# Expert weights by halves over 21 places, one buffer of gathered tokens, and a new order at the start of the expert stage

## The reference

```
h = rms_norm(x, norm_ffn)
choose one of 4 groups by router, in it 2 of 8 experts   # 32 experts in all
for each expert e, for the tokens that chose it:
    y = (silu(h @ w_gate[e]) * (h @ w_up[e])) @ w_down[e]  # 1024 -> 512 -> 1024
x = x + sum over the two experts of weight * y
x = rms_norm(x, norm_final)
```

## Time and profile before

| | |
|---|---|
| median of 3 runs | 964.09 us |
| the profiled execution | 965.7 us |
| its span, first to last instruction | 964.5 us |
| granted TensorE clock over the span | 0.993 |
| PE busy | 927.3 us, 96% |
| DVE, ACT busy | 455.5 us, 356.7 us |
| bytes moved by DMA | 291.88 MB, 303 GB/s over the span |

### The profile page before, as it was taken

One profiled execution on the slowest core, in us unless ns is written; L12 is line 12 of the kernel. 1 busy time (PEld: TensorE's weight loads), 2 busy tenths in 40 slices (PEclk: granted clock), 3 DMA queues, 4 the chain that ended last, 5 costly groups with the idle time before them and its releaser, 6 DMA issues.

```text
span 964.5 us, 12359 instructions
## 1 busy us (share of the span) xinstructions
PE 927.3 (96%) x4961; PEld 614.3 (64%) x4961; DVE 455.5 (47%) x775; ACT 356.7 (37%) x577; POOL 24.6 (3%) x41
## 2 busy tenths in 40 slices
PE   7999999999999999999999999887999989999997
PEld 6979889885444443444434433333999878888886
DVE  5878665445232322313222222213776667776444
ACT  7634555432221121221212211115654456665332
POOL 1400000000000000000000000000000000000000
PEclk9989999999999999999999999999999999999999
DMA  9954454596999999999999999999844535555401
GB/s 371 395 217 150 172 175 158 232 378 265 399 427 429 424 430 427 425 429 427 428 428 426 429 425 427 427 431 418 337 141 165 180 130 192 177 190 200 174 1 45
DMA packets 30685, 291.88 MB, mean 303 GB/s; under 512 B 5025, under 2 KB 5665, under 8 KB 7714
## 3 DMA queue, kind: packets, MB, share of 16 engines
q1 hardware_dynamic: 30194, 290.89, 74.8%
q10 hardware_dynamic: 432, 0.17, 0.1%
HBM read 290.00 MB, written 1.05 MB: 302 GB/s over the span
## 4 chain that ended last, share of the span: by engine, by line
PE 83%; DMA 10%; DVE 4%; ACT 1%; issue 1%; POOL 0%; SPq 0%; DVEq 0%; ACTq 0%
PE bank L1644 19%; PE bank L451 11%; PE bank L452 11%; PE bank L453 11%; PE bank L1666 10%; PE bank L2196 6%; DMA ring<-in_w_gate_up_second 5%; DMA ring<-in_w_gate_up_first 4%; PE bank L1616 3%; PE bank L2198 3%; PE bank L1682 3%; DVE w_low L547 1%; DMA head<-in_head 1%; PE bank L768 1%; PE bank L815 1%
## 5 line engine op out<-in xcount | busy, mean ns | idle before, releaser
L547 DVE TENSOR_TENSOR w_low<-ring,w_high 128x2048 fp32r<-128x2048 f32 x76 | 173.9, 2290 | 90.7 <-ACT w_high L515 90.4
L1644 PE MATMUL bank<-ring,arena 128*64 128x512 f32 x928 | 206.9, 595 | 7.3 <-DMA ring<-in_w_gate_up_second 5.3
L515 ACT ACTIVATE w_high<-ring 128x2048 fp32r<-128x2048 f32 x76 | 145.5, 1916 | 128.2 <-PE bank L453 94.2
L1644 PEld LDWEIGHTS bank<-ring,arena 128*64 128x64 f32 x928 | 64.9, 137 | 134.4 <-issue 118.3
L1781 DVE SCALAR_TENSOR_TENSOR y_low<-bank,arena,y_high 64x512 fp32r<-64x512 f32 x64 | 48.0, 750 | 137.8 <-ACT y_high L1716 137.4
L1666 PE MATMUL bank<-ring,arena 128*64 128x512 f32 x464 | 106.0, 598 | 4.4 <-issue 4.4
L2196 PE MATMUL bank<-xT_low_high,w_high 128*128 128x512 f32 x256 | 90.6, 399 | 1.3 <-DVE xT_low_high L558 1.1
L1716 ACT ACTIVATE y_high<-bank,arena 64x512 fp32r<-64x512 f32 x64 | 43.7, 683 | 125.8 <-PE bank L1666 125.3
L1772 DVE TENSOR_TENSOR arena<-bank,arena 128x256 f32<-128x256 f32 x32 | 13.6, 425 | 147.3 <-ACT arena L1703 147.3
L1703 ACT ACTIVATE arena<-bank 128x256 f32<-128x256 f32 x32 | 12.3, 385 | 190.8 <-PE bank L1644 190.8
L2198 PE MATMUL bank<-xT_low_high,w_low 128*128 128x256 f32 x256 | 71.8, 280 | 0.0
(11 more groups left out here) (317 smaller groups left out, 1617.7 us busy)
## 6 DMA issues: line engine op xcount, KB each, us to landing
ring<-in_w_down SPq DMA_DIRECT2D x28, 2048.0 KB, 27.5
ring<-in_w_gate_up_first SPq DMA_DIRECT2D x27, 2048.0 KB, 23.7
ring<-in_w_gate_up_second SPq DMA_DIRECT2D x27, 2048.0 KB, 25.2
ring<-in_dense_second SPq DMA_DIRECT2D x48, 1024.0 KB, 4.8
ring<-in_dense_first SPq DMA_DIRECT2D x28, 1024.0 KB, 6.2
extra_piece<-in_w_down SPq DMA_DIRECT2D x3, 2048.0 KB, 22.3
extra_piece<-in_w_gate_up_first SPq DMA_DIRECT2D x3, 2048.0 KB, 26.4
extra_piece<-in_w_gate_up_second SPq DMA_DIRECT2D x3, 2048.0 KB, 32.0
```

What stands on the lines that cost most here:

```text
L515: SC.activation(parts[buffer[0][u]][0][:, :], lanes[n % len(lanes)], ACT.Copy).then_inc(*high.inc(u))
L547: DVE.tensor_tensor(p[1][:, :], lanes[n % len(lanes)], p[0][:, :].bitcast(F32), ALU.subtract).then_inc(*split.inc(u))
L1644: last = PE.matmul(GU[t * SLOTS:(t + 1) * SLOTS, 0:NGU], xs[:, k, :], wgu[:, :, c, t * (DE // JT):(t + 1) * (DE // JT)], start=k == 0, sto ...
```

## The change

1. **Places.** The 18 halves of the nine slots, the two halves of `extra` and one unit in arena 0 make 21 places of 1 MB, each with its own semaphore. The first ten pieces are still loaded whole (the tenth is now expert 3's first gate-and-up piece). A load into arena 0 follows, after X and the low rows have been read there. From then on all loads are units of 1 MB, in the order in which PE reads them, each waiting for the read 21 units earlier.
2. **One buffer.** The gathered tokens of all groups of four lie in arena 2. Its layout alternates between groups, so that piece p of the next group goes where expert p of this one was read. The copies out wait for that expert's gate and up, and ACT makes its copy after the hidden copy.
3. **Order at the start.** Piece 0 is gathered whole, then piece 1; the low rows of tokens 128 to 255 are made in two halves. PE multiplies gate and up of expert 1 ahead of w_down of expert 0. Expert 1 moves from the steps into the begin functions.
4. **The second block's places move.** Its dense lanes lie in slots 0, 1, 8 and 2, split parts and other buffers in slots 3 to 6. All first eight dense units are issued as places come free, and `norm_final` after them, when gate and up of the last expert are done. Several semaphores of the first block are used again in the second.

```diff
@@ places
+PLACES = 2 * RING + 3
+    def place_words(place):
+        if place == PLACES - 1:
+            return arena[0][:, :]
+        whole = ring if place < 2 * RING else extra
+        return whole[:, place % (2 * RING) * UNIT:(place % (2 * RING) + 1) * UNIT]
@@ first_sync
-        early_piece(RING, w_down, 3, unit1.at("om2"))
+        early_piece(RING, w_first, 3, unit1.at("om2"))
         early_piece(5, w_down, 2, unit1.at("om3"))
+        SP.wait_ge(rows_summed, 1)
+        SP.wait_ge(*rows_low_done.at(1))
+        SP.dma_start(place_words(PLACES - 1), w_second[3][:, 0:UNIT]).then_inc(place_sem[PLACES - 1], 16)
@@ token_rows_low
+            for o in (slice(0, D // (1 + h)), slice(D // 2, D))[:1 + h]:
+                DVE.scalar_tensor_tensor(out=low[:, h, o], in0=X[:, h, o], scalar=stat("ffn", h),
...
@@ gathered tokens
-    XTE = [arena[i][:, 0:KC * FOUR * SLOTS].rearrange("p (c s) -> p c s", c=KC) for i in (2, 0)]
+    GATHERED = arena[2][:, :]
+    def gathered(layout, p, experts):
+        if layout == 0:
+            block = GATHERED[:, p * 512:(p + 1) * 512].rearrange("p (e c s) -> p c e s", e=FOUR, c=2)
+        else:
+            block = GATHERED.rearrange("p (e q c s) -> p q c e s", e=FOUR, q=NPIECES, c=2)[:, p, :, :, :]
+        return block[:, :, 0:experts, :]
@@ loads and reads by units
+    ORDER = [(n, j) for pair in ((0, 1),) for part in (range(4), range(4, 6)) for n in pair for j in part]
+    ORDER += [(n, j) for n in range(2, NE) for j in range(6)]
+    def gate_up_quarters(n, quarters_):
+        for j in quarters_:
+            PE.wait_ge(*landed(n, j))
+            gate_up(q, n, place_words(place_of(n, j)), n // FOUR % 2, n % FOUR, j, read_signal(n, j))
+    def expert_load(n, j):
+        SP.wait_ge(*has_read(*ORDER[ORDER.index((n, j)) - PLACES]))
+        src, half = ((w_first, w_second, w_down)[j // 2][n], j % 2)
+        place = place_of(n, j)
+        SP.dma_start(place_words(place), src[:, half * UNIT:(half + 1) * UNIT]).then_inc(place_sem[place], 16)
@@ tensor_begin, from the third quarter of expert 0
+        gate_up_quarters(0, (3,))
         gather_even(q, 1, 0)
-        PE.wait_ge(*q.at("routeT", 1))
-        turn_hidden(q, 0)
-        turn_route(q, 1, 0, 1, 1, GU)
-        PE.wait_ge(place_sem[dn], 16)
-        down(q, 0, piece(dn), 0, first_down_half)
+        turn_route(q, 1, 0, 1, 1, DN)
+        PE.wait_ge(*q.at("hidden", 1))
+        gate_up_quarters(1, (0, 1))
+        turn_hidden(q, 0)
+        gate_up_quarters(1, (2, 3))
+        PE.wait_ge(*q.at("routeT", 2))
+        down(0)
+        gather_odd(q, 1, 1)
+        turn_hidden(q, 1)
+        turn_route(q, 2, 1, 0, 2, GU)
+        down(1)
@@ vector_begin
+        routeT_out(q, 1, 0, 1, 0, DN)
+        hidden_out(q, 1)
+        y_low_out(q, 0, 0, 0)
+        build_route(q, 2, 1, -2)
+        xT_odd_out(q, 1, 1, 1, GATH, 2)
+        routeT_out(q, 2, 1, 0, -1, GU)
+        y_low_out(q, 1, 0, 1)
@@ after the last expert load
-    SP.wait_ge(*q.at("down", NE - 3))
-    for u in order2[0:2]:
+    for u, read in zip(order2[0:8], ORDER[ORDER.index((NE - 4, 4)):]):
+        SP.wait_ge(*has_read(*read))
         load_second(u)
-    SP.wait_ge(*q.at("gate_up_first", NE - 2))
-    for u in order2[2:4]:
-        load_second(u)
-    SP.wait_ge(*q.at("gate_up", NE - 1))
+    SP.wait_ge(*q.at("gate_up", NE))
     load_row("norm_final", a["norm_final"].rearrange("(l n) -> l n", l=1))
-    SP.wait_ge(*q.at("down", NE - 2))
-    for u in order2[4:6]:
-        load_second(u)
-    for u in order2[6:8]:
-        load_second(u)
```

More of the change, by code:

```diff
@@ L1635, in turn_route, with gate_up @@
         last.then_inc(*q.inc("turned"))
[L1637 to L1642, removed]
+    def gate_up(q, n, words, layout, e, quarter, signal):
+        w = words.rearrange("p (c m n) -> p m c n", c=2, m=2)
+        xs = gathered(layout, quarter, FOUR)[:, :, e, :]
+        for c in range(2):
+            k = 2 * quarter + c
             for t in range(JT):
-                last = PE.matmul(GU[t * SLOTS:(t + 1) * SLOTS, 0:NGU], xs[:, k, :],
-                                 wgu[:, :, c, t * (DE // JT):(t + 1) * (DE // JT)], start=k == 0, stop=k == KC - 1,
+                last = PE.matmul(GU[t * SLOTS:(t + 1) * SLOTS, 0:NGU], xs[:, c, :],
+                                 w[:, :, c, t * (DE // JT):(t + 1) * (DE // JT)], start=k == 0, stop=k == KC - 1,
                                  tile_position=(0, t * SLOTS), skip_group_check=True)
-        if KC // 2 - 1 in chunks_:
-            last.then_inc(*q.inc("gate_up" if half else "gate_up_first"))
-        return last
+        last.then_inc(*signal)
     def turn_hidden(q, n):
@@ L1656, in turn_hidden, with down_half @@
         last.then_inc(*q.inc("hidden_turned"))
[L1658 to L1663, removed]
+    def down_half(q, n, words, odd, half, signal):
+        if half == 0:
+            PE.wait_ge(*q.at("hiddenT", n + 1))
+            PE.wait_ge(*q.at("y", n))
+        wd = words.rearrange("p (c n) -> p c n", n=D)
+        for c in range(K4 // 2):
+            k = half * K4 // 2 + c
             o = (k % HCH) * P + (k // HCH) * SLOTS
@@ new lines, in build_program, with place_of, landed, read_signal @@
+    FIRST_PLACES = [2 * slot + half for slot in (6, 7, 0, 1, 8, 2, 3, 4, 5, RING) for half in range(2)] + [PLACES - 1]
+    WHOLE = PLACES - 1
+    def place_of(n, j):
+        return FIRST_PLACES[ORDER.index((n, j)) % PLACES]
+    def landed(n, j):
+        turn, at_ = divmod(ORDER.index((n, j)), PLACES)
+        if turn == 0:
+            return place_sem[FIRST_PLACES[at_ - at_ % 2]], 16
+        return place_sem[FIRST_PLACES[at_]], 16 * (turn if at_ < WHOLE and at_ % 2 else turn + 1)
+    def read_signal(n, j):
+        if j == 3:
+            return q.inc("gate_up")
+        if j == 5:
+            return q.inc("down")
+        return (first_down_half, 1) if j == 4 else (quarters, 1)
@@ L1824, in tensor_step @@
     def tensor_step(n):
-        s, four, buffer, pair, odd = n % FOUR, n // FOUR, n // FOUR % 2, n // 2, n % 2
+        s, four, pair, odd = n % FOUR, n // FOUR, n // 2, n % 2
         b = pair % 3
-        first, second, dn = places_of(n)
-        value_first, value_second, value_dn = landed(n)
         for p in pieces_at(n):
@@ L1837, in tensor_step @@
         PE.wait_ge(*q.at("routeT", n + 1))
[L1838 to L1844, removed]
-            gate_up(q, n, second, buffer, s, 1, (0, 1)).then_inc(quarters, 1)
-            gate_up(q, n, second, buffer, s, 1, (2, 3))
-        else:
-            gate_up(q, n, second, buffer, s, 1)
+        gate_up_quarters(n, range(4))
         for p in pieces_at(n):
```

219 lines of the change are left out of this document (88 added, 131 removed).

## The result

The changed kernel takes 978.52 us (median of 4 runs, 975.18 to 978.77) against 964.06 us for the kernel before (4 runs, 963.83 to 966.66). The comparison gives a ratio of 1.0109 with a 95% interval of 1.0086 to 1.0132: slower, by some 1.1%. These two medians lie farther apart (1.5%), because the four runs of the kernel before are near the low end of its spread: in the three later comparisons its median is 967.3 to 968.0 us over 19 to 23 runs, and 978.52 is 1.1% above that. The profiled execution took 978.56 us, its span 977.2 us, 12.7 more than before.

The account below looks back on a forecast made before the run. The one saturated DMA queue was taken to bound the expert stage. Restart -2.8, packets +6.0 and row +4.8 summed to +8.0 us: 973.7 us for the profiled execution, 972.1 on the median, range 966 to 977.

Parts of the forecast that it names:

- Frame: Expert stage: it ends when its bytes have gone through the one saturated DMA queue; PE has 10.3 us of slack.
- Packets: Expert weight loads: halves with 8 KB rows transfer 1.5% slower than whole pieces with 16 KB rows, +6.0 us.
- rival C: Halves cost 2.6% as dense units do, and the wait for expert 2's route its full time: +13.6 us, 977.7; chance 0.08.
- The row: Second block's start: norm_final queues behind eight dense units, lands late, and PE stalls ahead of q0, +4.8 us.
- The restart: Queue's pause near 225 to 252 us: twenty-first place, earlier gather and new expert order let loads resume sooner, -2.8 us.
- the route wait: Ahead of down 1, PE idles 2 to 3 us for expert 2's route; the queue pauses 0.9 us.
- The tail: End of the expert stage: halves gain nothing, because ACT takes y_high only after w_high of the first dense unit; 0.
- (E): Releases at the start don't come earlier because PE waits for the new order, gain 0: +10.8 us, 974.9; chance 0.07.
- (A): The queue pays for bytes alone, so loading by halves costs nothing: +2.0 us, 966.1; chance 0.13.
- (B): norm_final is in time or DVE's delay is absorbed, but halves cost: +3.2 us, 967.3; chance 0.10.
- (D): Outstanding transfers share the engines, so norm_final lands around 670 and halves cost nothing: faster, 960.8 us; chance 0.07.

Follow-up runs that it names:

- e1: Kernel before, with the 81 whole pieces of experts 5 to 31 loaded as two halves back to back; 973.30 us, ratio 1.0057.
- e3: Changed kernel, with DVE building expert 2's route ahead of y_low of expert 0; 976.80 us, ratio 1.0104 to the kernel before.
- e4: Changed kernel, with norm_final issued after four dense units and expert 2's route built ahead of y_low; 969.49 us, ratio 1.0017 to the kernel before.
- e7: Kernel before, pieces of experts 5 to 31 as two halves, each laid out contiguously in memory; 976.16 us, one run.
- e8: Kernel before, pieces of experts 5 to 31 loaded as four quarters (4 KB rows) back to back; 984.21 us, one run.
- e2: Changed kernel, with norm_final issued after four dense units instead of eight; 972.83 us, ratio 1.0057 to the kernel before.
- e6: e5 with arena 0 used once as a twenty-first place, for expert 3; 964.96 us, ratio 0.9976 to the kernel before.
- e9: e6 with expert 5 also by halves, whole pieces from expert 6; 966.83 us, ratio 1.0001 to the kernel before.
- e10: e9 with the last units also by halves and ACT's y_high ahead of w_high of v0.0; 968.95 us, ratio 1.0020 to the kernel before.
- e5: e4 with whole pieces from expert 5 on, twenty places and the second block's buffers where they were before; 968.69 us, ratio 1.0007 to the kernel before.

## Why the prediction came out as it did

**Frame: right.** The one queue ends the stage. The plateau moved the end by its own slowdown in e1, and PE's slack did not cover it.

**Packets, +6.0: right, with some luck.** 6.4 in e1. The 1.5% from two 6 us windows was the right row; 2.6% from the dense stretch (rival C) was not. With 350 and 176 packets the small windows could not carry two digits, as the prediction says itself; that 280 us of e1 give the same 1.5% is partly chance.

**The row, +4.8: right mechanism, too large by 1.5.** The row landed 21 us behind the last w_down, not 22, and its reader was itself later relative to H, since PE stood 3.25 us and then ran at 1.2 GHz for 3.4 us. DVE waited 3.3 us instead of 5.0.

**The restart, -2.8: the step that failed.** The prediction put it at 2.8, with the route wait priced as time in which PE stands, "PE starts expert 2 about 2 us later". Measured from A, nearly all its dates hold. It put the end of down 0 34.7 us behind A, measured 254.67 - 219.78 = 34.9. The route's arrival was put at 38.8, measured 39.0; the wait "2 to 3 us", measured 2.74. Then it gave down 1 its 3.65 us. It took 6.45: in 259 to 266 us the granted clock is 0.57 on average, so most of that stretch ran at 1.2 instead of 2.4 GHz, and PE had stood before it fell. Down 1's releases thus came at 43.3 and 46.1 us behind A, not 41.3 and 43.1; the 2 to 3 us missing there are the gain. Without that wait (e3, e4) the clock stays at 1.00 there and 3.7 us are gained. What costs the queue 3.4 us had been priced at 0.9. The Trainium skill, "TensorE: Matmul & The Clock Gate", section "Part 1: The HAM clock gate", says that the array's clock is halved after idleness. By that rule the same 16 matmuls take up to twice 3.65 us, an estimate of 7.3, and the trace agrees with 6.45. The prediction weighed what stood behind the wait, but took every duration from rows at full clock.

**The tail, 0: short by 0.5.** By halves PE still waits for y_high behind w_high, as said. The 3.25 us idle there is followed by 3.4 us at 1.2 GHz, and the scatter and the first turns run through it (H to v0.0 on PE: 8.45 us before, 8.97 after). This is the clock's doing and not that of the halves or of the longer wait alone: e7 waits as long there as e1 and the kernel before, and its clock falls (0.57 on average in 677 to 681 us; 1.00 in e1 in 675 to 679). First e1, then e7:

```profile
674.69 0.50 PE L1682 MATMUL bank<-y_high,routeT 128*128 128x512 f32 x1 [1.55 <-DVE y_low L1781]
```

```profile
675.93 0.50 PE L1683 MATMUL bank<-y_high,routeT 128*128 128x512 f32 x1 [1.55 <-DVE y_low L1782]
```

**The first stage: not in the sum.** A differs by 2.6 us, but not by the change. Kernels with the first stage of the kernel before have A at 215.86 (e8), 217.75 (e1), 219.33 (e7), those with the changed kernel's at 215.91 (e3), 217.15 (e2), 219.78 (after), and it goes with the granted clock in 50 to 70 us: 0.91, 0.83 and 0.74 in each of the two groups. The kernel before has 0.83 there. First after, then e8:

```profile
50.00:70.00 20.00, 18.21 (x73) 12.84 (x72) 13.74 (x29) 7.11 (x13) 0.00 (x0) 0.74 0.48 193
```

```profile
50.00:70.00 20.00, 18.22 (x103) 14.62 (x101) 15.69 (x34) 8.11 (x18) 0.00 (x0) 0.91 0.53 200
```

The sum, measured minus forecast: +2.5 restart, +0.4 packets, -1.5 row, +0.5 tail, +2.6 first stage, +0.2 behind q0 = +4.7, which is 12.7 - 8.0. Of the profiled execution's overshoot more than half is thus a draw of the first stage. Its other executions were not traced, but two of the three have nearly the same mean clock and time (0.986, 978.49 and 978.77 us, beside 0.987 and 978.56 of the traced one), and the third has a higher clock and is shorter (0.993, 975.18 us). Taken over the medians instead, 978.52 against the 967.3 to 968.0 us of the later comparisons is 10.5 to 11.3 us, and what is missing from the forecast's 8.0 (2.5 to 3.3 us) is about what the restart did not give (2.5).

**Rivals.** (E), no gain at the restart, is what came, though by another mechanism: the releases did come early, and were given back. (A) is refuted by e1, (B) by e2, and (D) by both costs: the row landed at 691.6, not near 670, and e1 pays for its rows. (C)'s price was near the measured median for the wrong reason.

## What to carry to other kernels

When a change adds a wait on TensorE, look at how long the engine will stand, and price the next work at half clock as a second case: here 2.74 us of standing cost another 2.8 us on the next 16 matmuls, and moving four small DVE operations ahead of one y_low won it all back. In a saturated queue, splitting transfers is paid in rows, for ever, while finer release is earned only where the queue runs dry. Splitting only there helps less than it seems, because the first large transfer after it must wait for two reads at once and opens the hole again. And whatever is moved in an ordered queue, list every small transfer that ends up behind it.

## What was not expected of the hardware

- Where the clock fell, and where it did not. It fell to 1.2 GHz behind waits of PE of 2.74 us (after, e2; for 6.8 us) and of 3.25 to 3.26 us (after, e2, e3, e4; for 3.4 us), but not behind the 3.08 us ahead of q0 in after. At the restart it never fell behind 1.53 us (six traces, e3 to e6, e9, e10). Ahead of the last scatter a wait of 1.55 us (1.69 in e8) stands in eight traces: behind it the clock fell for 3.4 us in e5, e7, e8 and e10, and not in before, e1, e6 and e9. So the length of the single wait does not decide by itself; what does, these runs do not show.
- The first stage varies by up to 3.9 us between kernels with the same code in it (A at 215.91 in e3, 219.78 after), in step with the granted clock near 53 us, behind a PE wait of 1.8 to 2.0 us that is there each time. That would be much of the 6 us spread of the kernel before (963.9 to 970.2 us in 21 runs), which was not traced run by run; of these 21 the three below 965 us have a mean granted clock of 0.997 or 0.998, all others 0.991 to 0.994.
- With some 27 us of transfers outstanding, SP's issues themselves take long: of the eight dense units (20.26 us in all) the first takes 6.30 us and six take 2.13 each, where 0.33 us is usual at the restart. In the kernel before single dense issues take up to 5.02 us. The prediction's 0.33 us per issue, taken from the restart, did not hold here; it did not enter its sum.
